# A mixture-of-experts kernel's last expert: earlier rows combined between two weight products, and the running sum carried into PSUM by identity products

## The reference, cut to what matters

```
x = x + mixing(rms_norm(x, norm_mix))
h2 = rms_norm(x, norm_ffn)
top_val, top_idx = top_k(h2 @ w_router + b_router, 4);  gates = softmax(top_val)
for expert e (32 of them), rows xe that chose it:
    gt = min(xe @ w_gate[e] + b_gate[e], 7);  up = clip(xe @ w_up[e] + b_up[e], -7, 7)
    ye = ((up + 1) * gt * sigmoid(1.702 * gt)) @ w_down[e] + b_down[e]
x = x + sum over the row's experts of gate * ye
y = rms_norm(x, norm_final)
```

## Time and profile before

| | |
|---|---|
| median of 3 runs | 1222.55 us (1222.38 to 1223.22) |
| profiled execution, its own time | 1223.54 us |
| its span, first to last instruction | 1221.6 us |
| PE busy | 1187.9 us, 97% of the span |
| DVE busy | 453.2 us, 37% |
| ACT busy | 199.4 us, 16% |
| HBM read | 424.92 MB, 352 GB/s over the span |
| mean granted PE clock | 0.997 of 2.4 GHz |

### The profile page before, as it was taken

How to read it: one execution, slowest core, us unless ns; L and a number is a source line. 1 busy time by engine, 2 the same in 40 slices (tenths; PEclk the granted TensorE clock), 3 DMA queues, 4 the chain that set the end, 5 groups by cost and what they waited for, 6 DMA issues and landing times.

```text
span 1221.6 us, 19136 instructions
## 1 busy us (share of the span) xinstructions
PE 1187.9 (97%) x8044; PEld 535.9 (44%) x8044; DVE 453.2 (37%) x993; ACT 199.4 (16%) x437; POOL 30.8 (3%) x34
## 2 busy tenths in 40 slices
PE   8999999999999999999999999999999999999995
PEld 6676799764333333333333333333333333333332
DVE  6899442253533322222322333322222222222224
ACT  3345323123101000100100001100010000001002
POOL 0000050030000000000000000000000000000000
PEclk9999999999999999999999999999999999999998
DMA  9524000398999999999999999999999999999994
GB/s 261 178 69 184 11 4 13 90 383 329 429 425 424 428 426 428 428 429 428 428 429 428 427 429 429 428 428 429 428 429 428 427 428 429 428 429 428 427 428 155
DMA packets 53596, 430.25 MB, mean 352 GB/s; under 512 B 12175, under 2 KB 25919, under 8 KB 28702
## 3 DMA queue, kind: packets, MB, share of 16 engines
q1 hardware_dynamic: 53314, 428.91, 85.1%
q10 hardware_dynamic: 228, 0.55, 0.1%
HBM read 424.92 MB, written 4.48 MB: 352 GB/s over the span
## 4 chain that ended last, share of the span: by engine, by line
PE 66%; DMA 19%; DVE 1%; ACT 1%; issue 0%; POOL 0%; DVEq 0%
PE bank L1856 41%; DMA ring<-in_w_up_dram 19%; PE bank L1834 6%; PE bank L1910 5%; PE bank L1096 3%; PE bank L1841 2%; PE bank L1181 2%; PE bank L1785 2%; PE bank L1461 1%; PE bank L1864 1%; PE bank L1051 1%; PE bank L1077 1%; PE bank L1882 1%; PE bank L1234 0%; PE bank L1230 0%; PE bank L1139 0%
## 5 line engine op out<-in xcount | busy, mean ns | idle before, releaser
L1856 PE MATMUL bank<-ring,arena 128*64 128x512 f32 x1536 | 342.2, 594 | 7.5 <-DMA ring<-in_w_up_dram 6.8
L1856 PE MATMUL bank<-arena 128*64 128x512 f32 x1536 | 342.5, 593 | 6.1 <-DMA arena<-in_w_up_dram 6.0
L1856 PEld LDWEIGHTS bank<-ring,arena 128*64 128x64 f32 x1536 | 109.1, 137 | 218.9 <-issue 200.6
L1856 PEld LDWEIGHTS bank<-arena 128*64 128x64 f32 x1536 | 108.9, 136 | 216.9 <-issue 199.4
L2131 DVE TENSOR_SCALAR arena<-bank 128x512 f32<-128x512 f32 x32 | 22.1, 692 | 380.2 <-PE bank L1864 380.2
L2145 DVE TENSOR_TENSOR arena<-arena,bank 128x512 f32<-128x512 f32 x186 | 113.7, 679 | 1.6 <-PE bank L1910 1.6
L540 PE MATMUL bank<-arena,ring 128*128 128x336 f32 x352 | 102.8, 447 | 0.3 <-ACT arena L357 0.3
L1910 PE MATMUL bank<-arena 64*128 64x512 f32 (+1 forms) x384 | 91.1, 606 | 0.7 <-issue 0.7
L1834 PE MATMUL bank<-arena 128*64 128x512 f32 (+1 forms) x384 | 89.5, 600 | 0.1
L2135 DVE TENSOR_SCALAR arena<-bank 128x512 f32<-128x512 f32 x32 | 22.1, 692 | 176.4 <-PE bank L1864 176.4
L540 PEld LDWEIGHTS bank<-arena,ring 128*128 128x128 f32 x352 | 65.8, 189 | 33.9 <-issue 2.5
(11 more groups left out here) (359 smaller groups left out, 784.6 us busy)
## 6 DMA issues: line engine op xcount, KB each, us to landing
ring<-in_w_gate_dram SPq DMA_DIRECT2D x32, 2048.0 KB, 24.5
arena<-in_w_up_dram SPq DMA_DIRECT2D x32, 2048.0 KB, 27.6
ring<-in_w_down_dram SPq DMA_DIRECT2D x32, 2048.0 KB, 31.0
arena<-in_w_gate_dram SPq DMA_DIRECT2D x32, 2048.0 KB, 26.3
ring<-in_w_up_dram SPq DMA_DIRECT2D x32, 2048.0 KB, 28.8
arena<-in_w_down_dram SPq DMA_DIRECT2D x31, 2048.0 KB, 30.7
ring<-in_w_in_dram SPq DMA_DIRECT2D x11, 1024.0 KB, 7.9
ring<-in_w_out_dram SPq DMA_DIRECT2D x4, 1024.0 KB, 8.1
```

The source lines that it names most:

```text
L1856: mm = M.matmul(bank[64 * hb:64 * hb + 64, b, :], tokens(cc), w[:, c, 512 * hb:512 * hb + 512], start=(cc == 0), stop=(w3 == 2 and cc == K ...
```

## The change: what it does

It touches the last expert and what follows it.

1. In the last expert PE combines expert 30's rows between the gate and the up product, no more behind the up product; DVE adds them to `acc` between its two clips, no more at the end of `glu`.
2. PE then brings the finished `acc` of experts 0 to 30 into the output banks by products with the identity (`seed`, one for each of the six pieces: `start=True, stop=False`). Three (k = 0, 4, 5, banks 5, 6, 7) stand between the up product and `turn_act`, after a wait for all six additions. Two (k = 1, 2) stand behind the down product, one (k = 3, bank 2) behind the wait for `ys`, all in front of the last `combine`, whose products now add to the banks (`start=False`).
3. With the sum in the banks, `add_tile` falls away. ACT squares the two banks of a tile, and DVE scales out of the banks in two instructions of 512 columns in place of one of 1024, after a wait for all six pieces (`cmb_done`).
4. ACT loads the table for the square root before it copies the last down product, no more after.
5. Where there are overflow blocks, the banks are copied to `acc` first; with these inputs that doesn't run.

```diff
--- before.py
+++ after.py
@@ -1661,6 +1663,9 @@
                     if first:
                         act.wait_ge(F["gt_turned"], 1)
                         A.copy(gT32, bank[:, 6, 0:NT]).then_inc(F["gt_ready"], 1)
+                    if last:
+                        act.wait_ge(F["eps_set"], 1)
+                        A.activation(small[:, 50:51], eps_fin, ACT.Sqrt)
                     take_down(at)
...
@@ -1677,13 +1682,11 @@
                         body(counter(it, GROUP, r))
...
                 for r in range(GROUP):
                     body(counter(NGROUP - 1, GROUP, r), last=(r == GROUP - 1))
-                act.wait_ge(F["eps_set"], 1)
-                A.activation(small[:, 50:51], eps_fin, ACT.Sqrt)
-
-                def norm(i):
+
+                def norm(i, rows):
                     n = TILES[i][1]
-                    A.activation(fin_junk[0:n, :], acc[0:n, i, :], ACT.Square, accum_out=small[0:n, 40 + i:41 + i])\
-                        .then_inc(F["fin_sq"], 1)
+                    A.activation(fin_junk[0:n, :].rearrange("p (c n) -> p c n", c=2), rows, ACT.Square,
+                                 accum_out=small[0:n, 40 + i:41 + i]).then_inc(F["fin_sq"], 1)
...
                 for i in range(3):
-                    act.wait_ge(F["cmb_read"], 6 * (NE - 1) + 2 * i + 2)
-                    norm(i)
+                    b = min(CMB_BANKS[2 * i:2 * i + 2])
+                    act.wait_ge(F["cmb_done"], 6 * (NE - 1) + 2 * i + 2)
+                    norm(i, bank[0:TILES[i][1], b:b + 2, :])
                     root(i, i + 1)
...
@@ -1882,10 +1886,12 @@
                         mm = M.transpose(bank[:, 3, i * P:i * P + m], Pg[0:m, i, :, :], ident[0:m, 0:m])
                     mm.then_inc(F["pgt_done"], 1)
 
-                def gate_up(at, over):
+                def gate_up(at, over, first=False, between=None):
 
                     pe.wait_ge(F["x_ready"], at(1, 1))
                     product(at, 0, 0, lambda cc: xT[:, cc % 4, cc // 4, :], 0, over).then_inc(F["g_done"], 1)
+                    if between:
+                        between()
                     product(at, 2, 1, lambda cc: xT[:, cc % 4, cc // 4, :], 1, over).then_inc(F["u_done"], 1)
...
-                def combine(at, biased=False):
+                def seed(k):
+
+                    i, hb = k // 2, k % 2
+                    t0, m = TILES[i]
+                    M.matmul(bank[0:m, CMB_BANKS[k], :], ident[0:m, 0:m], acc[0:m, i, 512 * hb:512 * hb + 512],
+                             start=True, stop=False)
+
+                def combine(at, biased=False, seeded=False):
 
                     pe.wait_ge(F["ys_ready"], at(1, 1))
                     pe.wait_ge(F["pgt_ready"], at(1, 1))
+                    if seeded:
+                        seed(3)
...
@@ -1908,18 +1923,28 @@
                         i, hb = k // 2, k % 2
                         t0, m = TILES[i]
                         M.matmul(bank[0:m, bk, :], PgT[64 * hb:64 * hb + 64, i, 0:m], ys[64 * hb:64 * hb + 64, :],
-                                 start=not biased, stop=True).then_inc(F["cmb_done"], 1)
+                                 start=not (biased or seeded), stop=True).then_inc(F["cmb_done"], 1)
 
                 def body(it, r, first=False, second=False, last=False):
                     at = counter(it, GROUP, r)
                     before = counter(it, GROUP, r - 1)
                     over = (r, it * (16 * PER // NSLOT))
-                    gate_up(at, over)
-                    if not first:
+
+                    def earlier_rows():
+
                         if not second:
                             pe.wait_ge(F["cmb_read"], before(6, 0))
                         combine(before, biased=second)
+
+                    gate_up(at, over, False, earlier_rows if last else None)
+                    if not first:
+                        if not last:
+                            earlier_rows()
                         pe.wait_ge(F["cmb_read"], before(6, 1))
+                    if last:
+                        pe.wait_ge(F["cmb_read"], before(6, 6))
+                        for k in (0, 4, 5):
+                            seed(k)
...
@@ -1972,8 +1997,10 @@
                         body(it, r)
                 for r in range(GROUP):
                     body(NGROUP - 1, r, last=(r == GROUP - 1))
-                pe.wait_ge(F["cmb_read"], 6 * (NE - 1))
-                combine(counter(NE - 1))
+                seed(1)
+                pe.wait_ge(F["pgt_ready"], NE)
+                seed(2)
+                combine(counter(NE - 1), seeded=True)
                 pe.wait_ge(F["tab_ready"], 1)
...
-                def glu(at, step):
+                def glu(at, step, between=None):
                     dve.wait_ge(F["g_done"], at(1, 1))
                     V.tensor_scalar(t1, bank[:, 0, :], LIMIT, None, ALU.min).then_inc(F["t1_ready"], 1)
                     dve.wait_ge(F["sg_ready"], at(1, 1))
                     V.tensor_tensor(sg, t1, sg, ALU.mult)
+                    if between:
+                        between()
                     dve.wait_ge(F["u_done"], at(1, 1))
                     V.tensor_scalar(u1, bank[:, 1, :], LIMIT, -LIMIT, ALU.min, ALU.max).then_inc(F["mstep"], 1)
...
                         make_p(rank_next)
-                    glu(at, at(1, 1))
-                    if not first:
-                        add_rows(counter(it, GROUP, r - 1))
+                    earlier = counter(it, GROUP, r - 1)
+                    glu(at, at(1, 1), (lambda: add_rows(earlier)) if last else None)
+                    if not first and not last:
+                        add_rows(earlier)
...
-                def add_tile(i):
-                    m = TILES[i][1]
-                    for k in (2 * i, 2 * i + 1):
-                        dve.wait_ge(F["cmb_done"], last_at(6, k + 1))
-                        o = acc[0:m, i, 512 * (k % 2):512 * (k % 2) + 512]
-                        V.tensor_tensor(o, o, bank[0:m, CMB_BANKS[k], :], ALU.add).then_inc(F["cmb_read"], 1)
-
-                def scale(i, k):
+                def scale(i, k, rows):
                     n = TILES[i][1]
                     dve.wait_ge(F["fin_root"], k)
                     link(V.reciprocal(small[0:n, 44 + i:45 + i], small[0:n, 36 + i:37 + i]))
-                    V.scalar_tensor_tensor(fin[0:n, i, :], acc[0:n, i, :], small[0:n, 44 + i:45 + i], gfin[0:n, :],
-                                           ALU.mult, ALU.mult).then_inc(F["fin_ready"], 1)
-
-                add_tile(0)
-                add_tile(1)
-                scale(0, 1)
-                add_tile(2)
-                scale(1, 2)
-                scale(2, 3)
+                    for hb in range(2):
+                        last = V.scalar_tensor_tensor(fin[0:n, i, 512 * hb:512 * hb + 512], rows(i, hb),
+                                                      small[0:n, 44 + i:45 + i], gfin[0:n, 512 * hb:512 * hb + 512],
+                                                      ALU.mult, ALU.mult)
+                    last.then_inc(F["fin_ready"], 1)
+
+                def in_bank(i, hb):
+                    return bank[0:TILES[i][1], CMB_BANKS[2 * i + hb], :]
+
...
+                dve.wait_ge(F["cmb_done"], last_at(6, 6))
+                for i in range(3):
+                    scale(i, i + 1, in_bank)
...
```

More of the change, by code:

```diff
@@ L1466, in project_z, with over_blocks @@
                 mm.then_inc(F["zp_done"], 1)
-        def over_blocks(eng, body, after):
+        def over_blocks(eng, body, after, ahead=None):
             n_over = eng.value_load(blocktab[0:1, NBLK:NBLK + 1], min_val=0, max_val=NOVER)
             with eng.If(n_over > 0):
+                if ahead:
+                    ahead()
                 with eng.Fori(NE, NE + NOVER) as it:
@@ L1702, in again @@
                     for i in range(3):
-                        norm(i)
+                        norm(i, acc[0:TILES[i][1], i, :].rearrange("p (c n) -> p c n", c=2))
                         root(i, 4 + i)
@@ L2204, in scale, with in_acc, keep_rows @@
                     link(V.reciprocal(small[0:n, 44 + i:45 + i], small[0:n, 36 + i:37 + i]))
[L2205 to L2213 removed]
+                    for hb in range(2):
[5 more added lines that the diff above has]
+                    return bank[0:TILES[i][1], CMB_BANKS[2 * i + hb], :]
+                def in_acc(i, hb):
+                    return acc[0:TILES[i][1], i, 512 * hb:512 * hb + 512]
+                dve.wait_ge(F["cmb_done"], last_at(6, 6))
+                for i in range(3):
+                    scale(i, i + 1, in_bank)
+                def keep_rows():
+                    for i in range(3):
+                        for hb in range(2):
+                            V.tensor_copy(in_acc(i, hb), in_bank(i, hb)).then_inc(F["cmb_read"], 1)
                 def again():
@@ L2219, in again @@
                     for i in range(3):
-                        scale(i, 4 + i)
-                over_blocks(dve, over_body, again)
```

(2 more changed lines are left out.)

## The result

Twenty runs of each, on the same chips: 1224.97 us with the change (1222.88 to 1226.54), 1223.05 before (1221.82 to 1226.1). The ratio is 1.0015 with a 95% interval of 1.0008 to 1.0021: the change makes the kernel slower by 1.8 us, 1.0 to 2.6. I had forecast +0.9 and 1223.4 us, with a range of 1221.5 to 1224.6, as no measurable change: the measured time lies 0.4 above that range.

A forecast was written before the change was run, and what follows sets the result against it. Weight transfers bound the kernel until the last expert's second up unit lands at 1192.25, then the engines. Last `combine` +3.41 less 2.50 won at the end gave +0.9 us: 1223.4 us, range 1221.5 to 1224.6.

The forecast's parts named there:

- term 4: From the last `combine` to the last scale: additions gone, scales out of banks, 9.73 becomes 7.23, a gain of 2.50 us.
- no overlap at all: Bound on the end: a scale's two pieces at 0.69 each, three scales 0.6 us longer, a gain of 1.9.
- Terms 1 to 3: Last expert on PE: moved `combine` delays up product +1.77, three seeds bring transposes to +1.52, three more last `combine` to +3.41.
- `sw` no longer ends last: Before the transposes: DVE's `sw` ready at 1199.39, PE's seeds ending at 1200.44.
- A: Seeds around the down product at half price, 0.43 us (0.52 by a skill rule); sum -1.45, 1221.1 us; chance 0.10.
- C: Seeds' weight loads not overlapped, 1.24 us a seed; sum +3.2, 1225.75 us; chance 0.05.
- B: Second up unit lands later against PE, hiding all of the moved `combine`; sum -0.9, 1221.7 us; chance 0.12.
- D: Whole change faster by over 2.4 us, taking A and B together (-3.2); chance 0.04, other causes included.

The follow-up runs named there:

- e3: Changed kernel with the six seeds as one-pass bfloat16 products on other data; last gate bias to last scale 29.14 us, ratio 0.9991 to the kernel before.
- e2: Kernel before with all six seeds behind the down product and the new end, `combine` in its old place; gate bias to last scale 32.83 us, ratio 1.0019.
- e5: Changed kernel with a tile's banks in ascending order, each scale one 1024-column instruction; last gate bias to last scale 31.41 us, ratio 0.9998.
- e4: Kernel before with each scale split into two 512-column instructions out of SBUF; last gate bias to last scale 30.68 us, ratio 0.9996.
- e9: Changed kernel unaltered, a second look; last gate bias to last scale 31.79 us, ratio 1.0007 to the kernel before.
- e10: Kernel before unaltered, a second look; last gate bias to last scale 30.39 us.
- e6: Kernel before with the first two products of expert 30's `combine` between the last expert's up units; last gate bias to last scale 30.10 us, ratio 0.9984.
- e7: e6 plus two seeds between expert 29's up units, tile 2 kept in the banks; last gate bias to last scale 28.11 us, ratio 0.9975 to before.
- e1: Kernel before with only expert 30's `combine` and its additions moved, no seeds, old end; last gate bias to last scale 32.69 us, ratio 1.0005.
- e8: Same kernel as e1, profiled in another execution; last gate bias to last scale 31.00 us.

## Why the prediction was right and wrong

**The mechanism was right.** PE sets the end from the second up unit on, the moved `combine` is hidden in part, the seeds stick out on both sides of the down product, and the additions taken off DVE give back less than that. Each of the steps in the table above came in that order, e3 shows by the yardstick that the seeds' length decides the sign, and e2 that they cost the same elsewhere.

**The step that failed is term 4, the end behind the last `combine`.** I had written that the pair of 512-column instructions of a scale "costs what the single one did", by two additions of that size that took 1.20 to the next start. An addition is a TENSOR_TENSOR; the scale is a SCALAR_TENSOR_TENSOR, and two of these took 1.41 with 1.33 to the next start. One by one, in the changed kernel, the pieces of the scales and the last expert's additions (line, count, duration ns min/median/max, starts, forms):

```profile
L2229 DVE SCALAR_TENSOR_TENSOR arena<-bank,arena x6: 736/746/752, 1215.8 to 1219.5; 128x512 f32<-128x512 f32 x4, 80x512 f32<-80x512 f32 x2
L2174 DVE TENSOR_TENSOR arena<-arena,bank x6: 675/680/682, 1190.9 to 1193.9; 128x512 f32<-128x512 f32 x4, 80x512 f32<-80x512 f32 x2
```

A piece of a scale took 0.07 more than an addition of the same size, 0.13 for the pair. Three scales came to 4.63 and not 4.28, and the first reciprocal stood 2.98 behind the start of `combine` and not 2.95: together 0.38, so the gain was 2.12 and not 2.50. The bound on the other side, no overlap at all, had held it (1.9), but as a bound alone. e5, with the split undone, has an end of 7.24 behind `combine`, where my sum said 7.23. That reading a bank costs nothing more held (e4, e5): the whole 0.13 of a scale is the split. The rule of the Trainium skill that the prediction weighed here (VectorE: DVE Perf Modes, section The TRN2 errata: 58 fixed cycles from SBUF, 120 from PSUM) gave +1.5 for the sum, nearer to the +1.39 than mine, but for another reason: by it a split costs 0.06 and the bank 0.06 for each instruction (an estimate from its cycles at 0.96 GHz), and e4 and e5 show 0.13 and nothing. The same section adds that the 58 falls short and that about 150 fixed cycles were measured, by which a split would cost 0.16 (an estimate), nearer to the 0.13. One slip changes nothing: the first reciprocal could have come at 1.21 + 1.51 = +2.72, not +2.74, and waited for +2.95 in any case.

**Terms 1 to 3.** The moved `combine`: +1.77 forecast, +1.80 measured. The seeds: 0.86 by L565; in place 0.89 (2.68 for the first three, 5.36 for e2's six), and 0.93 for the second three (2.78, of which the forecast had 0.1 for the change of shape behind them). The first three brought +0.08 at the transposes; from there to the down product took 1.36 and not 1.44, so that this stood at +1.52 as forecast; the second three brought the +0.10 by which `combine` was late. That `sw` no longer ends last held, with 1.16 us to spare.

**The number and the range.** By the yardstick +0.9 was too small by 0.5, of which 0.4 is term 4 and 0.1 the seeds. From the predicted 1223.4 to the measured 1224.97 are 1.57, and these 0.5 are only a part of it. Another 0.5 is the base: the median of before, 1222.55 in three runs, was 1223.05 in twenty. The last 0.6 stays open: the ratio of the times says +1.8 and the yardstick +1.39, which the interval (+1.0 to +2.6) does not tell apart, and the ratio of e9 lies below the yardstick's. The range ended at 1224.6 because it held costs of the change alone and nothing for the base; 1223.05 + 1.39 = 1224.44 would have been inside. That the time did not move by the 2.4 us that I had called measurable held, but 0.2% was too coarse a limit: twenty runs of each gave an interval that is 0.13% wide.

**The rivals.** A, half-price seeds, is out, and the 0.52 of its estimate with it: a seed took 0.89. C, bare weight loads at 1.24 a seed, is out as well. B, more of the wait hidden, did not occur in full: in three more profiles in which the second up unit waited behind an untouched first one, PE had 1.09 to 1.14 us of slack there (e2, e4, e10), as in the first (4.57 between the units' starts less a unit's 3.46). But e6 shows an execution in which the second up unit stood 0.6 later behind the gate bias. There the moved `combine` would have cost about 1.2 and not 1.8, and the whole change about +0.8 (an estimate: 1.80 and 1.39, each less 0.59). So the cost of the change depends in part on the execution; how often such a one comes is not shown. D did not come.

## What to carry to other kernels

Moving an addition from a half-idle engine onto the one that sets the end pays only in slots where that engine waits: identity products of the same kind cost 0.89 us each next to the down product (e2), and two experts before the last their time had been absorbed by the end (e7). In a chain of semaphores, ask what ends last after the move: the moved `combine` delayed the up product by 1.8 and the end by 0.6. And price an instruction by rows of its own kind: an addition's 0.60 to the next start is not a scale's 0.67, and cutting a scale in two cost 0.13.

## What the runs showed that I had not expected

- The granted clock fell to half for 3.4 us inside the down product in one of two profiled executions of the same kernel (e1, not e8), after PE had idled 1.60 us for the activated rows and then done only transposes. It cost 1.7 us, more than the whole change by the yardstick. e8 had the same idle time and the same transposes and kept its clock, so they alone do not bring it; what else is needed is not shown.
- From the last gate bias on, two executions of the changed kernel agree to 0.01 us, and so do two of the kernel before (31.79 twice, 30.40 and 30.39), while the whole time spreads over 3 us. A local span told from two profiles each what twenty runs told with an interval of 1.6 us. It is no rule: e1 and e8, one kernel, differ by 1.69, and in e6 the transfer that the span hangs on came 0.6 later.
